# A mixture-of-experts stage: 32 slots in four column groups for small experts, three rounds for 129 to 192 tokens, and the expert biases laid over 128 rows

## The chip, the cores and the metric

The kernel runs on one NeuronCore of a Trainium2 chip. The metric is the device time of one execution in microseconds (us). TensorE (PE in the profile) does the matrix products, VectorE (DVE), ScalarE (ACT) and GpSimd (POOL) the rest, and SyncE (SP) issues the DMA transfers.

## What is computed

The input is one sequence of 256 tokens, 1024 wide, in float32. A first block applies a modulated mixer (windowed attention beside a linear recurrence) and then a mixture of experts; two layers of a second kind follow (three attention and pooling branches, then a gated feed-forward). The change touches the mixture of experts alone. Cut to what matters, with `h` the 256 tokens:

```python
logits = h @ w_router + b_router                 # 32 experts
top_vals, top_idx = lax.top_k(logits, 4)         # each token goes to 4 experts
gates = softmax(top_vals)
for each expert e, with the tokens xb that chose it:
    gu   = xb @ w_gu[e] + b_gu[e]                # 1024 -> 2048: gate half, up half
    gate = minimum(gu[:, :1024], 7.0)
    up   = clip(gu[:, 1024:], -7.0, 7.0)
    y    = ((up + 1.0) * gate * sigmoid(1.702 * gate)) @ w_down[e] + b_down[e]
    out[tokens] += y * gates
```

The weights of one expert are 1024 x 2048 and 1024 x 1024 float32 numbers, 12.58 MB. How many tokens an expert gets depends on the inputs. The reference's router, run on these inputs, gives for experts 0 to 31: 23, 7, 42, 55, 16, 24, 146, 18, 11, 55, 31, 4, 12, 57, 6, 15, 59, 61, 7, 52, 22, 9, 2, 52, 31, 1, 19, 75, 38, 26, 11, 37. So 20 experts have at most 32 tokens, ten have 33 to 64, expert 27 has 75 and expert 6 has 146.

## The kernel before

Every engine runs a program of its own, in an order written out by hand, and waits on semaphores. The mixture of experts is a loop over the 32 experts on PE, ACT, DVE and SP.

**Slots and rounds.** The tokens of an expert get slots 0, 1, 2, ... A round handles 64 slots (`FEW`). PE, ACT and DVE read the expert's count (`value_load`, L1093 on PE) and branch: one round for at most 64 tokens, two for at most 128, four for more. A semaphore that counts rounds goes up by `R // rounds` with `R` = 4, so that an expert always adds four.

**One round on PE** (`expert`, from L998). It begins with the bias (L1009): four products per round that write the whole of banks 0 (gate) and 1 (up). `bias_hi` and `bias_lo` hold the biases of 32 experts times two column halves over 64 rows, split into a high and a low part in the rounded type fp32r, and `bias_sel` picks the expert's rows. Then come the gate and up products (L1017): for each of 8 pieces `gu0` to `gu7` of the weights (1 MB each), for gate and up, two products of 64 slots by 512 columns, one into the first 64 partitions of the bank, one into the other 64. Each takes a different half of the weight columns, and they use different column groups of the array. A float32 product shows as two MATMUL rows. Then the middle: the previous expert's result is added into the accumulators (`combine`, L994), the gates are transposed (L1034), the next tokens are gathered (L980), the hidden values are transposed (L1050, four transposes) and the gathered tokens too (L987). Last comes the down product (L1068), 16 products of 64 by 512 over the pieces `dn0` to `dn3` (1 MB each).

**Around it.** ACT computes the sigmoids and copies banks to SBUF (L1490 to L1505). DVE clips and multiplies gate and up (L1939 to L1955, operations 256 columns wide), copies the transposed hidden values (L1958), and prepares selection tables for the next expert (`select`, `select_gates`, `select_bias`).

**The weights.** SP loads them into a ring of 12 slots of 1 MB, which is exactly one expert (`load_expert`, L630 for gate and up, L632 for down). A slot is refilled with the same piece of the next expert once PE has used it in the expert's **last** round:

```python
if final and k < DT - 1:
    last.then_inc(gu_used.sem, 1)        # PE, in the last round only
```

After the last expert the same queue loads the first weights of the next layer (8.3 MB) into slots that come free.

**Bias set-up.** Before the loop, SP loads the bias rows with two transfers (L619), ACT copies them rounded into `bias_hi` (L1466), DVE makes `bias_lo` (L1832).

Of the kernel before, what the change touches and what calls it, by code (L numbers as in the profile page):

```python
# [22 lines left out]
P = 128  # L23
T = 256
# [15 lines left out]
FEW = 64  # L40
LIMIT, ALPHA = 7.0, 1.702
# [9 lines left out]
ROUNDS = 4  # L51

# [108 lines left out]

def constants():
# [67 lines left out]
def build(nc, dram, out, stop=None):  # L230
# [12 lines left out]
    with ctx:  # L243
# [14 lines left out]
        bias_hi, bias_lo = sb("bias_hi", [P, 2, 512], F32R), sb("bias_lo", [P, 2, 512], F32R)  # L258
# [118 lines left out]
        bias_raw = lru_a.rearrange("p a b -> p (a b)")[0:2 * NE, :].rearrange("p (a b) -> p a b", a=2)  # L377
# [183 lines left out]

        block = ctx.enter_context(nc.Block())
# [3 lines left out]
        def _(sp):  # L566
# [183 lines left out]
        def _(pe):  # L750
# [220 lines left out]
            both = (slice(0, FEW), slice(FEW, P))  # L971

# [25 lines left out]
            def expert(e, rounds):  # L998

                u = R // rounds  # L1000
                for r in range(rounds):
                    final = r == rounds - 1

                    pe.wait_ge(xT_ready.sem, xT_ready.at(R + r * u, e))
                    if r == 0:
                        pe.wait_ge(sel_ready.sem, sel_ready.at(1, e))
                    for g in range(2):
                        for n, rows in enumerate((bias_hi, bias_lo)):
                            mm(psum[g], bias_sel[0:2 * NE].rearrange("p a b -> p (a b)"), rows[0:2 * NE, g, :], start=n == 0,  # L1009
                               stop=False, skip_group_check=True)  # L1010
                    for k in range(DT):
                        if r == 0:
                            pe.wait_ge(exp_in[f"gu{k}"].sem, exp_in[f"gu{k}"].at(16, e))
                        wt = piece(exp_stream, f"gu{k}", 2).rearrange("p g (c f n) -> p g c f n", f=2, n=P)
# [11 lines left out]
                    pe.wait_ge(y_ready.sem, y_ready.at(R + r * u, e))  # L1026
                    pe.wait_ge(sg_ready.sem, sg_ready.at(R + r * u, e))
# [16 lines left out]
                    pe.wait_ge(sg_ready.sem, sg_ready.at(R + (r + 1) * u, e))  # L1044
                    for h in range(2):
                        if h == 1:
                            pe.wait_ge(up_taken.sem, up_taken.at((r + 1) * u, e))
# [1292 lines left out]
```

## Time and profile before

| | us |
|---|---|
| median of 3 runs | 2229.58 (2224.77 to 2230.18) |
| profiled execution, its own time | 2224.29 |
| its span, first to last instruction | 2222.5 |
| PE busy | 2122.2 (95%) |
| DMA queue, share of the 16 engines | 67.9% |
| mean granted TensorE clock | 0.989 |

The span lies 1.8 us under the execution's own time. "Busy" counts an engine as busy while one of its instructions runs; PE is pipelined, so a busy PE is not PE at its peak. In the 40 slices of the page, the experts fill slices 4 to 22 (about 180 to 1240 us), and the GB/s row there reads 381 418 417 303 1 381 418 and on to 411. Numbers that the page gives for the whole span average over stages of very different kinds, so the prediction reads each stage by itself.

### The profile page before, as it was taken

What the parts mean: (1) busy time and instruction counts of PE and PEld (TensorE: products, weight loads), DVE (VectorE), ACT (ScalarE), POOL (GpSimd) and SP (SyncE); (2) the same over time, 40 slices, a digit from 0 to 9 for tenths busy, and PEclk for the clock granted to TensorE, in tenths of its full rate; (3) what the DMA queues carried; (4) which work ended last, traced back from release to release, by engine and by line L of the source; (5) the groups of instructions that cost most, each with busy time, mean ns of one, the idle gap of its engine ahead of it and who ended that gap; (6) DMA issues with size and microseconds to landing.
All of it is one profiled execution on the core that took longest, in us unless ns stands there. A gap on an engine that the chain in (4) does not pass through costs nothing.

```text
span 2222.5 us, 29751 instructions
## 1 busy us (share of the span) xinstructions
PE 2122.2 (95%) x11486; PEld 1333.1 (60%) x11487; DVE 812.7 (37%) x1468; ACT 540.9 (24%) x905; POOL 25.3 (1%) x45
## 2 busy tenths in 40 slices
PE   6998999999999999999999999999999999999999
PEld 4763333333333333333333787778999887688999
DVE  3521221122222112221121348434885258425874
ACT  1421111111111111111111122312663132403653
POOL 0000000000000000000000020000000020000000
PEclk8998999999999999999999999999999999999999
DMA  9686997099999999999899334316551633325551
GB/s 347 254 353 255 410 419 303 1 381 418 418 417 417 417 419 418 418 418 418 334 417 411 106 114 152 114 40 199 178 194 53 199 112 118 114 97 169 190 176 53
DMA packets 210004, 580.05 MB, mean 261 GB/s; under 512 B 23264, under 2 KB 124896, under 8 KB 173952
## 3 DMA queue, kind: packets, MB, share of 16 engines
q1 hardware_dynamic: 209920, 578.83, 67.9%
q8 instruction: 65, 1.06, 0.2%
q14 instruction: 19, 0.16, 0.0%
HBM read 577.48 MB, written 1.31 MB: 260 GB/s over the span
## 4 chain that ended last, share of the span: by engine, by line
PE 69%; DMA 10%; SPq 8%; DVE 8%; ACT 3%; issue 2%; ACTq 0%; DVEq 0%
PE bank L756 16%; PE bank L1017 13%; DMA ring<-in_w_gu 9%; PE bank L1068 8%; SPq L630 4%; SPq L632 4%; PE bank L1340 3%; PE bank L1342 3%; PE bank L1341 3%; PE bank L980 3%; PE bank L994 3%; DVE heap L2104 2%; PE bank L826 2%; DMA ring<-in_w_in 2%; PE bank L1356 1%
## 5 line engine op out<-in xcount | busy, mean ns | idle before, releaser
L1017 PE MATMUL bank<-ring,heap 128*64 128x512 f32 x2304 | 519.2, 601 | 23.9 <-DMA ring<-in_w_gu 23.8
L1017 PEld LDWEIGHTS bank<-ring,heap 128*64 128x64 f32 x2304 | 158.0, 138 | 367.2 <-issue 289.2
L756 PE MATMUL bank<-heap,ring 128*128 128x256 f32 (+1 forms) x1600 | 350.5, 380 | 5.3 <-DVE heap L2148 3.2
L756 PEld LDWEIGHTS bank<-heap,ring 128*128 128x128 f32 (+1 forms) x1600 | 301.0, 189 | 51.5 <-DVE heap L2148 4.0
L1939 DVE TENSOR_SCALAR heap<-bank 128x256 f32<-128x256 f32 x36 | 15.3, 425 | 744.9 <-PE bank L1017 744.9
L1068 PE MATMUL bank<-ring,heap 128*64 128x512 f32 x1152 | 255.1, 595 | 0.0
L1340 PE MATMUL bank<-h_hi,w_hi 128*128 128x256 f32 x640 | 181.7, 284 | 3.4 <-DVE w_lo L2161 3.4
L1342 PE MATMUL bank<-h_hi,w_lo 128*128 128x256 f32 x640 | 181.1, 283 | 0.0
L1341 PE MATMUL bank<-h_lo,w_hi 128*128 128x256 f32 x640 | 181.1, 283 | 0.0
L2161 DVE TENSOR_TENSOR w_lo<-ring,w_hi 128x2048 fp32r<-128x2048 f32 (+1 forms) x64 | 142.4, 2226 | 97.7 <-ACT w_hi L1635 97.7
L1068 PEld LDWEIGHTS bank<-ring,heap 128*64 128x64 f32 x1152 | 79.3, 137 | 150.2 <-issue 144.2
L1491 ACT ACT_TABLE_LOAD x32 | 41.1, 1283 | 485.5 <-DVE heap L1939 485.0
L1635 ACT ACTIVATE w_hi<-ring 128x2048 fp32r<-128x2048 f32 (+1 forms) x64 | 119.1, 1861 | 145.2 <-PE bank L1342 85.5
L1340 PEld LDWEIGHTS bank<-h_hi,w_hi 128*128 128x128 f32 x640 | 122.8, 192 | 3.9 <-DVE w_lo L2161 3.8
L1341 PEld LDWEIGHTS bank<-h_lo,w_hi 128*128 128x128 f32 x640 | 122.8, 192 | 0.1
L1342 PEld LDWEIGHTS bank<-h_hi,w_lo 128*128 128x128 f32 x640 | 122.8, 192 | 0.0
L1356 PE MATMUL bank<-f_hi,w_hi 128*128 128x256 f32 x352 | 100.0, 284 | 1.0 <-DVE w_lo L2161 1.0
L1357 PE MATMUL bank<-f_lo,w_hi 128*128 128x256 f32 x352 | 99.6, 283 | 0.0
L1358 PE MATMUL bank<-f_hi,w_lo 128*128 128x256 f32 x352 | 99.6, 283 | 0.0
L1505 ACT ACTIVATE heap<-bank 128x512 f32<-128x512 f32 x36 | 21.5, 598 | 231.5 <-PE bank L1068 231.5
L980 PE MATMUL bank<-heap 128*64 128x512 f32 x296 | 73.4, 617 | 3.5 <-DVE heap L1899 3.5
L994 PEld LDWEIGHTS bank<-heap 64*128 64x128 f32 x592 | 54.1, 186 | 35.8 <-issue 29.2
(299 smaller groups left out, 2321.9 us busy)
## 6 DMA issues: line engine op xcount, KB each, us to landing
ring<-in_w_gu SPq DMA_DIRECT2D x256, 1024.0 KB, 18.8
ring<-in_w_down SPq DMA_DIRECT2D x128, 1024.0 KB, 19.8
ring<-in_ffn_w_up SPq DMA_DIRECT2D x44, 1024.0 KB, 7.7
ring<-in_w_ada SPq DMA_DIRECT2D x24, 1024.0 KB, 10.6
ring<-in_w_in SPq DMA_DIRECT2D x24, 1024.0 KB, 7.9
ring<-in_ffn_w_down SPq DMA_DIRECT2D x16, 1024.0 KB, 6.0
ring<-in_w_in SPq DMA_DIRECT2D x7, 2048.0 KB, 12.2
ring<-in_w_out SPq DMA_DIRECT2D x6, 2048.0 KB, 12.8
```

What stands on the lines that cost most here:

```text
L756: last = mm(outp, w(k), x(k), start=k == 0, stop=k == nk - 1)
L980: last = mm(psum[2][both[f], :], pick[:, t, FEW * r:FEW * (r + 1)], htok[:, t, 512 * f:512 * (f + 1)], start=t == 0, stop=t == TT - 1)
L994: last = mm(acc_of(f, c), y_sb[both[f], P * c:P * (c + 1)], sgT[both[f], :], start=False, stop=True, skip_group_check=True)
L1017: last = mm(psum[g][both[f], :], xgT[:, k % 4, k // 4, :], wt[:, g, :, f, :], start=False, stop=k == DT - 1, skip_group_check=True)
L1068: last = mm(psum[2][both[f], :], hidT[:, o:o + FEW], wt[:, 512 * f:512 * (f + 1)], start=k == 0, stop=k == DT - 1)
L1340: mm(b[:, g, :], wh, h_hi[:, k, :], start=k == 0, stop=False)
L1341: mm(b[:, g, :], wh, h_lo[:, k, :], start=False, stop=False)
L1342: last = mm(b[:, g, :], wl, h_hi[:, k, :], start=False, stop=k == DT - 1)
L1356: mm(b[:, a, :], wh, f_hi[:, k, :], start=k == 0 and a == 0, stop=False, skip_group_check=True)
L1357: mm(b[:, a, :], wh, f_lo[:, k, :], start=False, stop=False, skip_group_check=True)
L1635: f(hi, src, ACT.Copy).then_inc(S["whi"].sem, 1)
L2161: v.tensor_tensor(lo, src, hi.bitcast(F32), ALU.subtract).then_inc(S["wlo"].sem, 1)
```

## The change

It has four parts.

1. Experts with at most 32 tokens get a branch of their own: 32 slots. Gate and up are computed by four products of 32 slots by 256 columns, each in a column group of its own (`quarter`), in place of two of 64 by 512. The bias of such an expert is made by eight float32 products of 256 columns. The hidden values then lie in 256 columns of 128 partitions and not in 512, so ACT and DVE work on 128 columns at a time and PE makes two transposes in place of four. The down product has 32 slots per product, and as many products and columns as before.
2. Experts with 129 to 192 tokens take three rounds (`turns` gives the semaphore steps 1, 1, 2) and not four.
3. The biases' high and low parts lie one above the other in one tile `bias_pair` of 128 rows, so that one product per bank adds both: two per round in place of four. It takes four bias transfers in place of two, and four small copies per expert in `select_bias` in place of two.
4. The branching is one helper, `by_count`, for the three engines, with the small counts first.

```diff
+FEWER = 32
+CLASSES = ((32, 1), (64, 1), (128, 2), (192, 3), (256, 4))
...
+def turns(rounds):
+    marks = {1: (0, 4), 2: (0, 2, 4), 3: (0, 1, 2, 4), 4: (0, 1, 2, 3, 4)}[rounds]
+    return [(r, a, b - a) for r, (a, b) in enumerate(zip(marks, marks[1:]))]
...
-        bias_hi, bias_lo = sb("bias_hi", [P, 2, 512], F32R), sb("bias_lo", [P, 2, 512], F32R)
+        bias_pair = sb("bias_pair", [P, 2, 512], F32R)
...
+            def among(classes):
+                (most, rounds), rest = classes[0], classes[1:]
+                if not rest:
+                    expert(e, rounds, most <= FEWER)
+                    return
+                with eng.If(n <= most):
+                    expert(e, rounds, most <= FEWER)
+                with eng.Else():
+                    among(rest)
...
-            for f in range(2):
-                sp.dma_start(bias_raw[NE * f:NE * (f + 1)].rearrange("e g (c n) -> e (g c) n", n=P),
-                             bias_rows.rearrange("e (b f n) -> f e b n", f=2, n=P)[f]).then_inc(bias_in.sem, 16)
+            for g in range(4):
+                sp.dma_start(bias_raw[NE * g:NE * (g + 1)].rearrange("e g (c n) -> e (g c) n", n=P),
+                             bias_rows.rearrange("e (b f n) -> f e b n", f=2, n=P)[g % 2]).then_inc(bias_in.sem, 16)
...
             both = (slice(0, FEW), slice(FEW, P))
+            quarter = [slice(FEWER * j, FEWER * (j + 1)) for j in range(4)]
...
                     for g in range(2):
-                        for n, rows in enumerate((bias_hi, bias_lo)):
-                            mm(psum[g], bias_sel[0:2 * NE].rearrange("p a b -> p (a b)"), rows[0:2 * NE, g, :], start=n == 0,
-                               stop=False, skip_group_check=True)
+                        if few:
+                            for f in range(2):
+                                for c in range(2):
+                                    mm(psum[g][quarter[2 * f + c], 0:T], bias_sel[:, f, 0:FEWER].bitcast(F32),
+                                       bias_pair.bitcast(F32)[:, g, :].rearrange("p (i c n) -> p i c n", c=2, n=P)[:, :, c, :],
+                                       start=True, stop=False, skip_group_check=True)
+                        else:
+                            mm(psum[g], bias_sel.rearrange("p a b -> p (a b)"), bias_pair[:, g, :], start=True, stop=False,
+                               skip_group_check=True)
...
                             for f in range(2):
-                                last = mm(psum[g][both[f], :], xgT[:, k % 4, k // 4, :], wt[:, g, :, f, :],
-                                          start=False, stop=k == DT - 1, skip_group_check=True)
+                                if few:
+                                    for c in range(2):
+                                        last = mm(psum[g][quarter[2 * f + c], 0:T], xgT[:, k % 4, k // 4, 0:FEWER],
+                                                  wt[:, g, :, c, f, :], start=False, stop=k == DT - 1, skip_group_check=True)
+                                else:
+                                    last = mm(psum[g][both[f], :], xgT[:, k % 4, k // 4, :],
+                                              wt[:, g, :, :, f, :].rearrange("p i c n -> p (i c) n"),
+                                              start=False, stop=k == DT - 1, skip_group_check=True)
...
+                    wide = 1 if few else 2
...
-                        for i in range(2):
+                        for i in range(wide):
...
+                        n = FEWER if few else FEW
                         for f in range(2):
-                            last = mm(psum[2][both[f], :], hidT[:, o:o + FEW], wt[:, 512 * f:512 * (f + 1)],
+                            last = mm(psum[2][FEW * f:FEW * f + n, :], hidT[:, o:o + n], wt[:, 512 * f:512 * (f + 1)],
...
-            v.tensor_tensor(bias_lo[0:2 * NE], bias_raw, bias_hi[0:2 * NE].bitcast(F32), ALU.subtract).then_inc(bias_ready.sem, 1)
+            v.tensor_tensor(bias_pair[2 * NE:P], bias_raw[2 * NE:P], bias_pair[2 * NE:P].bitcast(F32), ALU.subtract) \
+                .then_inc(bias_ready.sem, 1)
...
                 for f in range(2):
-                    ins = v.tensor_copy(bias_sel[0:2 * NE, f, :],
-                                        const("ident")[0:2 * NE, bass.ds(e + NE * f, 1)].to_broadcast([2 * NE, FEW]))
+                    for half in (slice(0, 2 * NE), slice(2 * NE, P)):
+                        ins = v.tensor_copy(bias_sel[half, f, :], const("ident", 2 * P)[half, bass.ds(e + NE * f + half.start, 1)]
+                                            .to_broadcast([2 * NE, FEW]))
...
-            def expert(e, rounds):
-                u = R // rounds
+            def expert(e, rounds, few):
+                w = P if few else T
```

How the instructions stand, first on PE at the start of an expert with one round, before (for every expert of at most 64 tokens), rows of one product each:

```order
L1009 MATMUL bank0<-bias_hi,bias_sel 128x512 [waits sel_ready]
L1009 MATMUL bank0<-bias_lo,bias_sel 128x512
L1009 MATMUL bank1<-bias_hi,bias_sel 128x512
L1009 MATMUL bank1<-bias_lo,bias_sel 128x512
L1013 ISA
L1017 MATMUL bank0<-ring,heap 64x512 [waits in_gu0]
L1017 MATMUL bank0<-ring,heap 64x512
L1017 MATMUL bank1<-ring,heap 64x512 x2
```

The same place in the change, for an expert of at most 32 tokens:

```order
L1039 MATMUL bank0<-bias_pair,bias_sel 32x256 [waits sel_ready]
L1039 MATMUL bank0<-bias_pair,bias_sel 32x256 x3
L1039 MATMUL bank1<-bias_pair,bias_sel 32x256 x4
L1047 ISA
L1053 MATMUL bank0<-ring,heap 32x256 [waits in_gu0]
L1053 MATMUL bank0<-ring,heap 32x256 x3
L1053 MATMUL bank1<-ring,heap 32x256 x4
```

A piece of weights takes eight products of 256 columns where it took four of 512, and the wait for the piece stands where it stood. The same place in the change for 33 to 64 tokens, where only the bias differs:

```order
L1043 MATMUL bank0<-bias_pair,bias_sel 128x512 [waits sel_ready]
L1043 MATMUL bank1<-bias_pair,bias_sel 128x512
L1047 ISA
L1056 MATMUL bank0<-ring,heap 64x512 [waits in_gu0]
L1056 MATMUL bank0<-ring,heap 64x512
L1056 MATMUL bank1<-ring,heap 64x512 x2
```

Then on PE the end of the middle and the start of the down product, in the change, for at most 32 tokens:

```order
L1092 MATMUL bank3<-consts_sb,heap 128x128 [waits hid_ready]
L1089 REGISTER_ALU [waits up_taken]
L1092 MATMUL bank1<-consts_sb,heap 128x128 [waits hid_ready]
L1016 MATMUL bank0<-consts_sb,heap 128x128 [waits x_ready,g_ready]
L1016 MATMUL bank0<-consts_sb,heap 128x128 x3
L1112 MATMUL bank2<-ring,heap 32x512 [waits in_dn0,hidT_ready]
L1112 MATMUL bank2<-ring,heap 32x512 x3
```

Each of the two transposes of hidden values was a pair before; the down products keep their number and their 512 columns.

## Rows read from the trace of the kernel before

**Rows 1.** By stretch: busy us (instructions) per engine, PEclk, DMA share, GB/s; the experts' weights.

```profile
core 0: us, PE busy (x) PEld busy (x) DVE busy (x) ACT busy (x) POOL busy (x), PEclk, DMA share, GB/s
188.40:375.70 187.30, 179.01 (x854) 66.58 (x852) 33.56 (x94) 26.41 (x43) 0.00 (x0) 0.97 0.99 403
375.70:448.60 72.90, 72.29 (x360) 27.78 (x358) 12.43 (x32) 8.79 (x18) 0.00 (x0) 1.00 0.01 1
448.60:1083.40 634.80, 605.21 (x2910) 219.35 (x2908) 123.45 (x346) 90.27 (x152) 0.00 (x0) 1.00 1.01 416
1083.40:1092.60 9.20, 9.20 (x44) 3.20 (x42) 0.00 (x0) 0.60 (x1) 0.00 (x0) 1.00 0.00 0
```

**Rows 2.** The same view, one round each: experts 0, 2 and 22.

```profile
181.60:215.00 33.40, 30.00 (x135) 11.12 (x134) 5.70 (x16) 4.19 (x7) 0.00 (x0) 0.91 0.80 320
245.50:273.20 27.70, 27.44 (x136) 10.34 (x134) 5.70 (x16) 4.19 (x7) 0.00 (x0) 1.00 1.02 419
...
907.60:937.80 30.20, 28.27 (x137) 9.99 (x135) 5.70 (x16) 4.19 (x7) 0.00 (x0) 1.00 1.02 418
```

**Rows 3.** Chain of waits, 340 to 480 us (start, length, what): expert 6's last round.

```profile
444.42 1.12 PE bank L1009 x4
445.53 13.88 PE bank L1017 x64
459.42 1.93 PE bank L994 x16
...
465.00 7.02 PE bank L1068 x32
```

**Rows 4.** The same view, 1040 to 1240 us: expert 27, and the last expert's end.

```profile
1048.94 24.86 DMA ring<-in_w_gu
1073.84 1.94 PE bank L1017 x8
...
1088.43 1.13 PE bank L1009 x4
...
1219.75 7.04 PE bank L1068 x32
1226.87 0.61 ACT heap L1505
...
1237.84 2.37 PE bank L1163 x11
```

**Rows 5.** Timeline (start, length) at expert 0: its gate and up products, the first refills.

```profile
183.62 15.60 PE L1017 MATMUL bank<-ring,heap 128*64 128x512 f32 x64
...
187.40 12.33 SPq L630 DMA_DIRECT2D ring<-in_w_gu  x8
```

**Rows 6.** Timeline of PE: products of 256 columns, and the transposes of hidden values.

```profile
1248.03 28.11 PE L756 MATMUL bank<-ring 128*128 128x256 f32 x128
...
264.75 0.66 PE L1050 MATMUL bank<-consts_sb,heap 128*128 128x128 f32 x4
```

**Rows 7.** Timeline of PE: four column groups in the mixer's modulation; short products.

```profile
17.88 3.64 PE L795 MATMUL bank<-ring,vec 128*32 128x512 f32 x32
...
117.30 0.27 PE L893 MATMUL bank<-heap 128*64 128x128 f32 x1
...
117.47 0.27 PE L892 MATMUL bank<-heap 128*64 128x128 f32 x1
```

**Rows 8.** By stretch, columns as in rows 1: the DMA engines before the bias copy.

```profile
133.90:139.10 5.20, 5.20 (x45) 1.97 (x38) 2.88 (x5) 1.31 (x3) 0.00 (x0) 1.00 0.00 1
```

**Rows 9.** Timeline of ACT: the copy of the biases.

```profile
138.70 1.05 ACT L1466 ACTIVATE bias_hi<-heap 64x1024 fp32r<-64x1024 f32 x1
```

**Rows 10.** Waits, 180 to 1240 us: us in total, times, longest.

```profile
PE bank L1009 <- issue: 6.7, 2, 3.5
```

**Rows 11.** By stretch, columns as in rows 1: the modulation, paced by its weights.

```profile
21.60:26.40 4.80, 2.13 (x16) 0.31 (x16) 1.49 (x5) 0.00 (x0) 0.00 (x0) 1.00 1.03 428
26.40:31.60 5.20, 3.87 (x16) 0.40 (x16) 0.00 (x0) 0.36 (x1) 0.00 (x0) 0.51 1.01 381
```

More of the change, by code:

```diff
@@ L996, in combine @@
                 return last
-            def expert(e, rounds):
-                u = R // rounds
-                for r in range(rounds):
+            def expert(e, rounds, few):
+                for r, at, u in turns(rounds):
                     final = r == rounds - 1
-                    pe.wait_ge(xT_ready.sem, xT_ready.at(R + r * u, e))
+                    pe.wait_ge(xT_ready.sem, xT_ready.at(R + at, e))
                     if r == 0:
@@ L1514, in _ @@
             with act.Fori(0, NE) as e:
-                n = act.value_load(counts_i[0:1, bass.ds(e, 1)], min_val=0, max_val=T)
-                with act.If(n > P):
-                    expert(e, 4)
-                with act.Else():
-                    with act.If(n > FEW):
-                        expert(e, 2)
-                    with act.Else():
-                        expert(e, 1)
+                by_count(act, e, expert)
             for i in range(4):
@@ L1925, in _, with expert @@
             v.tensor_copy(small_done, gsum[:, 0, 0:1]).then_inc(slots_ready.sem, 1)
-            def expert(e, rounds):
-                u = R // rounds
-                c = Chain(dve, e_chain, e)
-                for r in range(rounds):
+            def expert(e, rounds, few):
+                w = P if few else T
+                for r, at, u in turns(rounds):
                     final = r == rounds - 1
                     if final:
-                        dve.wait_ge(x_full.sem, x_full.at(R + r * u, e))
+                        dve.wait_ge(x_full.sem, x_full.at(R + at, e))
                         select(e + 1).then_inc(pick_ready.sem, 1)
-                    dve.wait_ge(gate_full.sem, gate_full.at((r + 1) * u, e))
-                    v.tensor_scalar(act_g[:, 0:T], psum[0][:, 0:T], LIMIT, None, ALU.min).then_inc(g_ready.sem, u)
-                    v.tensor_scalar(act_g[:, T:2 * T], psum[0][:, T:2 * T], LIMIT, None, ALU.min).then_inc(g_ready.sem, u)
-                    dve.wait_ge(g_ready.sem, g_ready.at((2 * r + 2) * u, e))
-                    dve.wait_ge(up_full.sem, up_full.at((r + 1) * u, e))
-                    for h in range(2):
-                        part = slice(T * h, T * (h + 1))
+                    dve.wait_ge(gate_full.sem, gate_full.at(at + u, e))
+                    for h in range(2):
+                        part = slice(w * h, w * (h + 1))
+                        v.tensor_scalar(act_g[:, part], psum[0][:, part], LIMIT, None, ALU.min).then_inc(g_ready.sem, u)
+                    dve.wait_ge(g_ready.sem, g_ready.at(2 * (at + u), e))
+                    dve.wait_ge(up_full.sem, up_full.at(at + u, e))
+                    for h in range(2):
+                        part = slice(w * h, w * (h + 1))
                         ins = v.tensor_scalar(act_u[:, part], psum[1][:, part], LIMIT, -LIMIT, ALU.min, ALU.max)
@@ L1965, in _ @@
             with dve.Fori(0, NE) as e:
-                n = dve.value_load(counts_i[0:1, bass.ds(e, 1)], min_val=0, max_val=T)
-                with dve.If(n > P):
-                    expert(e, 4)
-                with dve.Else():
-                    with dve.If(n > FEW):
-                        expert(e, 2)
-                    with dve.Else():
-                        expert(e, 1)
+                by_count(dve, e, expert)
             dve.wait_ge(route_in.sem, 48)
```

73 lines of the change are left out of this document (35 added, 38 removed).

## The prediction

> **What bounds the kernel now.** I read the experts' stage in the view by stretch, because the page's average (PE 95% busy) mixes stages. While the weights of the experts stream, the DMA engines run at their limit: from 448.6 to 1083.4 us their share is 1.01 at 416 GB/s [rows 1]. That stretch holds the weights of 21 experts (7 to 27), so one expert costs the queue 634.8 / 21 = 30.23 us, a piece of 1 MB 30.23 / 12 = 2.52 us. A round on PE takes 27.7 us when all is there, and 30.2 us where PE waits for pieces [rows 2]. So an expert with one round is bound by its weights, and PE is the faster of the two by only 2.5 us.
>
> The reader is to see next where the queue stands still: 72.9 us from 375.7 to 448.6 at 1 GB/s, and 9.2 us from 1083.4 to 1092.6 [rows 1]. The ring holds one expert, and a slot is refilled only in the expert's last round. The first gap is expert 6 with its four rounds, the second expert 27 with two. Twice, then, PE sets the pace: in the gaps, and in the five rounds behind the second gap, 27.7 us each, until the last expert ends at 1226.9 [rows 4].
>
> From this I take a rule for the sum: the end moves by what the gaps of the queue shrink, plus what the tail saves, and a faster round elsewhere is worth nothing, since 30.23 us per expert stays.
>
> **A round in parts.** Expert 6's last round [rows 3]: bias 1.12, gate and up 13.88, middle 465.00 - 459.42 = 5.58, down 7.02 us; with what lies between, 27.6.
>
> **The change, term by term.**
>
> *Gate and up with 32 slots.* 64 products of 256 columns, two MATMUL rows each, four side by side: 32 steps. Four column groups do run side by side here: in the modulation 32 rows of 512 columns take 3.64 us, 0.114 each, where two groups in the experts take 13.88 / 64 = 0.217 [rows 7, 3]. A row of 256 columns takes 28.11 / 128 = 0.22 us alone [rows 6], so 32 x 0.22 = 7.0 us in place of 13.88: -6.9. Above, the bound is 13.9 (no more side by side than today); by the modulation's rate it would be 128 rows x 0.114 / 2 = 7.3. Issue asks for a product's row each 0.055 us; four short rows at 117.30 to 117.47 start 0.057 apart [rows 7] (two more stand between the two shown), so it can just be done in a burst.
>
> *Bias.* Two of the four products of 1.12 us go for 33 slots and more. Half would be 0.56, but part of it is the lead-in, so -0.47, and a round of 27.1 to 27.2. For 32 slots there are eight float32 products, four steps of 0.22 and a start: about 1.05, no change.
>
> *Middle.* Two of four transposes of 0.66 / 4 [rows 6] go: -0.3 at most, DVE and ACT get shorter operations that PE hides already. Down stays at 7.02, for it still has 512 columns. A round of 32 slots is then 27.6 - 6.9 - 0.3 = 20.4 us.
>
> *Start of the stream.* The first refill waits for piece 0 of expert 0, computed at half clock from 183.62 and released at 187.2 [rows 5]. Expert 0 has 23 tokens, so this takes 1.8 us, not 3.6: -1.8. Up to 375.7 the queue needed 187.3 us for 72 pieces, which at 2.52 are 181.4: 5.9 us were lost while PE, in experts 0 and 1 at clock 0.91, released too late [rows 1, 2]. With 20 us rounds for both (7 tokens in expert 1) I leave 0.5 of it: -5.4. The stream now stands still from 368.5.
>
> *Expert 6, three rounds.* Its first round now waits for its weights. A first round that does ends 5.0 us after the stream stands still (1088.4 against 1083.4 [rows 4, 1]), so at 373.5. A middle round of 27.1 brings 400.6; the last round releases piece 0 after bias and a piece, 0.65 + 1.7 us, and the stream runs 1.35 later (444.4 + 1.1 + 1.75 against 448.6 before). It restarts at 404.3, against 448.6: **-44.3**. Of this 27.6 is the round that goes, 0.5 to 1 the bias, the rest the earlier arrival at expert 6.
>
> *Experts 7 to 26.* The queue still needs 634.8 us: 1039.1. No gain, no loss, as long as rounds stay under 30.2.
>
> *Expert 27 and the tail.* Second round at 1044.1, restart at 1044.1 + 3.7 = 1047.8, four more experts 120.9 us: 1168.7, and the last expert ends 5.0 later, at **1173.7**. PE alone would need 1044.1 + 3 x 27.2 + 2 x 20.4 = 1166.5, so the tail changes sides: it now waits for weights. Against 1226.9 this is **-53**.
>
> *What hides the rest.* The two added bias transfers (128 KB each): the engines are idle from 133.9 to 139.1, and ACT's copy runs at 138.7 [rows 8, 9]; cover gone, they would cost at most their own 1 to 2 us. Two more small DVE copies per expert lie under PE's down product. The next layer's weights come behind the last expert's (8.3 MB, 20 us, now 1168.7 to 1188.7); the first of them must be there 11 us after the last expert's end (1237.84 - 1226.87 [rows 4]), at 1184.7, and lands 4 us behind 1168.7. If later pieces were late, I would give it 5 us.
>
> **Sum.** Profiled execution 2224.29 - 53 = 2171.3. The median of the runs, 2229.58, lies 5.3 over that execution, so the median I forecast is **2176.5**.
>
> **Rivals.**
>
> *A. The small rounds are no cheaper in effect: -33.* Then only a round less for expert 6 (27.6) and 0.47 us in some 13 rounds that PE paces (6) remain: -33, 2196. This takes 7 us lost per small expert, and there are two ways. First, four groups do not gain over two; against it stands the modulation's row. Second, PE pauses and then runs slow. Small experts leave it idle: 0.9 us of work per 2.52 us piece. In the modulation PE worked 2.13 of 4.80 us waiting for weights, and then the granted clock was 0.51, the 1.2 GHz level, for the next 5.2 us [rows 11]. So I expect the clock to fall in these experts. What it costs falls in the middle and down part, dense work of 12.6 us; after the idle stretch at 215.0 expert 1's round, at mean clock 0.90, took 30.5 and not 27.7, thus about +3. Such a round ends late by 3, but the next expert has pieces waiting and catches up, since PE has 30.2 us: nearly hidden, 0 to 3 us in all. Only with a further pause does it add up to 7. A pause of about 3.5 us shows before the bias products twice, 6.7 us in all [rows 10], when a branch or the loop's start is first taken; later returns do not show it. The Trainium skill (Runtime: NRT & Kernel Launch, Instruction fetch mechanics) says that a taken branch whose target is not in the current window forces a fetch before execution goes on. By that rule each of the 18 changes of class between experts might pause; the trace before contradicts it for the loop's return, which happens 31 times with two pauses. In parts (3 to 6 us lost) the gain is 50 to 38.
>
> *B. Slower: the clock stays down in small experts.* If the whole small round ran at 1.2 GHz it would take 2 x 20.4 = 41 us, more than the queue's 30.2, and PE would set the pace throughout: 20 x 41 + 10 x 27.2 + 5 x 27.1 = 1228 us against 1045 before (1226.9 - 181.6), +183, 2412. It decides from (1045 - 407) / 20 = 31.9 us per small round on. For it: the clock row of the modulation. Against it: PE then had no idle time left, and in experts 0 and 1 the clock came back within the round [rows 2]. The Trainium skill (TensorE: Matmul & The Clock Gate, Loop structure matters more than you think) describes waiting for a DMA before each burst of products as the loop that makes PE run cold; by it alone all 20 small experts would run so, and the outcome would be B.
>
> *C. Nothing comes of it.* Were few experts small or none over 128 tokens, or were the queue never idle, time would stay at 2229. The 72.9 us gap speaks against the last, and the router's counts against the rest.
>
> **Chances.** Forecast, gain 45 to 60: 0.72. A, with its partial forms, gain 30 to 45: 0.20. B: 0.03. C: 0.02. More gain than 60: 0.03, for nothing in the queue can give it but a faster start. The range takes in the forecast and A's main part: low 2224.8 (the fastest run) - 59 = 2166, high 2229.6 - 36 = 2194. A measurement of this kernel can tell about 0.3%, 7 us, from no change. Faster by more: 0.95; within: 0.02; slower: 0.03.
>
> **What would show it.** In the view by stretch the gap of the queue at expert 6 should be about 36 us (368 to 404), and the one at expert 27 about 9 us. Experts 7 to 26 together should stay at 635 us whatever their class. The gate and up rows of a small expert with its weights there (experts 7 and 8) should take 7 us, starts 0.055 apart; the tail should show waits for in_w_gu, and the last expert should end near 1174. The clock should show 1.2 GHz stretches in small experts. The forecast is wrong if the second gap ends later than 1055, if a small round takes over 27 us without waiting for weights, or if bias products of many experts are preceded by pauses of 3 us.

## The result, and the profile after

The change makes the kernel slower: 2335.51 us (median of 4 runs, 2334.67 to 2336.77) against 2229.59, a ratio of 1.0485 [1.0471, 1.0499] (in brackets, here and below, the 95% interval). The forecast was 2176.5 us. The profiled execution took 2336.77 us, 112.5 more than the one of before, and the last expert now ends at 1339.5 us and not at 1226.9: all of it lies in the experts' stage.

The stage by stretch, cut where the queue of weights stands still, as in [rows 1]:

```profile
core 0: us, PE busy (x) PEld busy (x) DVE busy (x) ACT busy (x) POOL busy (x), PEclk, DMA share, GB/s
190.80:403.90 213.10, 170.92 (x1144) 63.97 (x1137) 35.02 (x116) 27.25 (x47) 0.00 (x0) 0.90 0.90 356
403.90:441.80 37.90, 37.70 (x183) 13.57 (x184) 4.50 (x12) 4.12 (x8) 0.00 (x0) 1.00 0.00 1
441.80:475.80 34.00, 23.42 (x122) 8.77 (x122) 6.17 (x18) 2.92 (x6) 0.00 (x0) 0.91 0.94 373
480.50:1184.80 704.30, 544.77 (x3766) 196.76 (x3760) 108.56 (x370) 84.23 (x146) 0.00 (x0) 0.88 0.91 359
1184.80:1193.50 8.70, 8.70 (x42) 2.89 (x40) 0.00 (x0) 0.60 (x1) 0.00 (x0) 1.00 0.02 3
```

The gap at expert 6 did shrink, from 72.9 to 37.9 us, as forecast (36). What broke is the steady rate. In 704.3 us the queue brings 20 experts, 35.2 us each where it was 30.2; its share is 0.91 where it was 1.01. PE is busy for 544.77 / 20 = 27.2 us per expert, where it was 605.21 / 21 = 28.8, so PE is not what holds it.

The queues in that stretch (packets, MB, share of the 16 engines), after:

```profile
q1 hardware_dynamic: 44797, 251.65, 90.3%
q14 instruction: 101, 0.83, 0.3%
q8 instruction: 3, 0.05, 0.0%
```

and before, from 448.6 to 1083.4 us, where nothing stands for queue 14:

```profile
q1 hardware_dynamic: 47035, 264.22, 101.4%
q8 instruction: 3, 0.05, 0.0%
```

So 101 blocks of 8 KB of program code are loaded in 20 experts, five per expert, on an instruction queue that was silent. Whose code it is, the queue's line does not say. A hint stands in VectorE's timeline around one expert's end (start, duration, line, operation, count, idle time before and its releaser):

```profile
582.03 1.00 DVE L1937 TENSOR_SCALAR heap<-consts_sb,heap 128x512 f32<-128x512 f32 x2
582.94 0.79 DVE L1946 CAST bias_sel<-consts_sb 64x64 fp32r x4
595.41 0.62 DVE L1930 TENSOR_SCALAR heap<-consts_sb,heap 128x256 f32<-128x256 f32 x2 [11.68 <-issue]
```

After the loop's return VectorE stands still for 11.68 us and waits for no semaphore; experiment 1 confirms that the code is its own. The waits of the stretch (us in total, times, longest) sum this up:

```profile
DVE heap L1930 <- issue: 247.5, 19, 16.1
PEld bank L1053 <- DMA ring<-in_w_gu: 161.0, 87, 3.9
PE bank L1053 <- DMA ring<-in_w_gu: 100.7, 79, 3.4
PE bank L1056 <- DMA ring<-in_w_gu: 47.3, 45, 2.3
```

VectorE's standstill is 247.5 / 19 = 13.0 us at the mean. PE waits for weights, and weights come later. The records of the landings show in what way: each piece of 1 MB lands in 16 parts. In one piece (issued at 568.50 us) the first part lands at 576.37, the fifteenth at 576.94 and the last at 590.70; before, a piece in the steady stretch (issued at 915.92) had its first at 934.01 and its last at 935.93. So one part of the 16 is behind, by 10 to 17 us in most pieces of the stretch, and PE can begin a piece only when its last part is there. Last landings follow each other by 2.5 us (median), as before, by 3.5 us where one code block is fetched between them, and by 4.4 where two are.

PE's small round itself came out as forecast. Expert 1, with its weights there, then an expert paced by its weights:

```profile
212.58 7.09 PE L1053 MATMUL bank<-ring,heap 128*32 128x256 f32 x128
...
595.18 1.42 PE L1053 MATMUL bank<-ring,heap 128*32 128x256 f32 x16 [3.29 <-DMA ring<-in_w_gu]
597.66 1.94 PE L1053 MATMUL bank<-ring,heap 128*32 128x256 f32 x16 [1.06 <-DMA ring<-in_w_gu]
601.18 1.94 PE L1053 MATMUL bank<-ring,heap 128*32 128x256 f32 x16 [1.58 <-DMA ring<-in_w_gu]
```

The 64 products take 7.09 us where two column groups took 13.88 [rows 3]. In the paced expert a piece takes 1.94 us of work in place of 7.09 / 8 = 0.9: the granted clock is 0.50, the 1.2 GHz level, from 600 to 610 us (0.88 on the mean of the whole stretch). This is hidden behind the wait for the next piece.

### The profile page after: what moved, and what is told of

It reads as the page before. It is cut to its first block, busy times and chain, and to the rows that moved or that the text cites. A ratio compares the mean times of both kernels' runs of the same rounds, so it can differ in the third digit from the quotient of the medians.

```text
span 2335.0 us, 32573 instructions
## 1 busy us (share of the span) xinstructions
PE 2041.2 (87%) x12802; PEld 1302.9 (56%) x12803; DVE 797.8 (34%) x1524; ACT 532.8 (23%) x899; POOL 25.4 (1%) x45
## 4 chain that ended last, share of the span: by engine, by line
PE 53%; DMA 20%; SPq 14%; DVE 7%; issue 3%; ACT 2%; ACTq 0%; DVEq 0%
DMA ring<-in_w_gu 19%; PE bank L784 16%; SPq L660 7%; SPq L658 6%; PE bank L1112 5%; PE bank L1056 3%; PE bank L1377 3%; PE bank L1379 3%; PE bank L1378 3%; DVE heap L2128 2%; PE bank L854 2%; PE bank L1023 2%; PE bank L1009 2%; PE bank L1053 2%; DMA ring<-in_w_in 1%
## 5 line engine op out<-in xcount | busy, mean ns | idle before, releaser
L1053 PE MATMUL bank<-ring,heap 128*32 128x256 f32 x2560 | 228.5, 498 | 129.6 <-DMA ring<-in_w_gu 129.5
L1056 PE MATMUL bank<-ring,heap 128*64 128x512 f32 x960 | 230.3, 616 | 64.6 <-DMA ring<-in_w_gu 62.1
L1112 PE MATMUL bank<-ring,heap 128*32 128x512 f32 (+1 forms) x1120 | 248.8, 595 | 3.3 <-DMA ring<-in_w_down 3.2
L1053 PEld LDWEIGHTS bank<-ring,heap 128*32 128x32 f32 x2560 | 87.1, 133 | 263.3 <-DMA ring<-in_w_gu 204.7
L1971 DVE TENSOR_SCALAR heap<-bank 128x128 f32<-128x128 f32 (+1 forms) x70 | 21.1, 343 | 499.4 <-PE bank L1053 269.6
L1056 PEld LDWEIGHTS bank<-ring,heap 128*64 128x64 f32 x960 | 63.4, 139 | 223.9 <-DMA ring<-in_w_gu 118.0
L1112 PEld LDWEIGHTS bank<-ring,heap 128*32 128x32 f32 (+1 forms) x1120 | 67.8, 121 | 158.8 <-issue 144.7
L1930 DVE TENSOR_SCALAR heap<-consts_sb,heap 128x256 f32<-128x256 f32 x66 | 20.3, 350 | 378.9 <-issue 377.6
```

The lines of the kernel that those rows point to most:

```text
L1053: last = mm(psum[g][quarter[2 * f + c], 0:T], xgT[:, k % 4, k // 4, 0:FEWER], wt[:, g, :, c, f, :], start=False, stop=k == DT - 1, skip_gr ...
L1112: last = mm(psum[2][FEW * f:FEW * f + n, :], hidT[:, o:o + n], wt[:, 512 * f:512 * (f + 1)], start=k == 0, stop=k == DT - 1)
```

## The experiments

**The theories.** Three causes are possible. F: VectorE's loop over the experts has become too long to be kept, so every expert fetches it again, and these fetches slow the weights. In the compiled programs the loop has 199 instructions before and 336 after (ScalarE 112 and 176, PE 1950 and 3174). P: PE's longer code, or its branches, make PE late. S: the small rounds are slow, by the low clock or by four products side by side. If F holds, then by what: the traffic of the fetches (F1), or VectorE's standstill of some 13 us per expert (F2)?

**1. Only VectorE longer.** The kernel before, with a branch in VectorE's loop that is never taken; a second run has two. PE's program is that of before.

```diff
-                with dve.If(n > P):
+                with dve.If(n > T - 1):
                     expert(e, 4)
                 with dve.Else():
-                    with dve.If(n > FEW):
-                        expert(e, 2)
+                    with dve.If(n > P):
+                        expert(e, 4)
...
```

> The kernel before, with one branch added to VectorE's loop that is never taken (four more rounds of code for a count of 256, which no expert has). Nothing that is executed changes but one compare and branch. VectorE's loop grows from 199 to 288 instructions and still lies within three blocks of 128. Theory F (VectorE's loop has outgrown what its sequencer keeps, its code is fetched again for every expert, and each fetch delays one of the 16 DMA engines that carry the weights): no change if three blocks fit, 2229 us, about 19 packets on instruction queue 14. Rival C (the low TensorE clock and the pauses of small experts make the changed kernel slow): 2229 us, no change. It is the control for the next run.

> The kernel before, with two such branches that are never taken: VectorE's loop has 377 instructions and reaches over four blocks of 128, as in the changed kernel (336). No small experts, no four column groups, four rounds for expert 6, old biases. Theory F: slower, about 5 us for each expert that waits for weights, 2330 to 2390 us; 60 to 160 more packets on instruction queue 14; the landings of one weight piece spread over 10 us instead of 2. Rival C: 2229 us, since nothing of the small experts is in it.

Measured: 2355.41 us, ratio 1.0584 [1.0559, 1.0610], with 288 instructions in the loop, and 2356.51, 1.0581 [1.0561, 1.0600], with 377. The first was meant as a control without a change, and that expectation failed. Its stretch of 21 experts and its queue 14:

```profile
462.80:1199.30 736.50, 618.78 (x2910) 214.23 (x2908) 123.57 (x346) 90.12 (x152) 0.00 (x0) 1.00 0.91 360
...
q14 instruction: 105, 0.86, 0.3%
```

736.5 / 21 = 35.1 us per expert, with PE's clock at 1.00 and no small round anywhere. This alone reproduces the loss, and P and S fall as its cause; experiment 5 is the test from the other side. The second dead branch adds nothing, and nothing to the fetches either: 105 packets in the same stretch. It adds to VectorE's standstill, though. That is 16.1 us per return at the mean in the first run and 19.4 in the second, at the same time per expert, which speaks against F2.

**2. Where the limit lies.** Dead branches with fewer rounds (239 and 264 instructions), and the changed kernel made shorter on VectorE: `select_gates` and `select_bias` once behind the branches in place of once in each (289), that with one copy in `select_bias` in place of four (283), and the change without its 32-slot class (292).

> The kernel before with one dead branch of one round in VectorE's loop: 239 instructions, between the 199 that keep the code and the 288 that do not. Theory F: either 2229 us or about 2350 us, and nothing between; if what is kept is two blocks of 128, or 256 instructions, it is fast.

> The kernel before with one dead branch of two rounds in VectorE's loop: 264 instructions. Theory F with a limit of 256 instructions: slow, about 2350 us and some 170 packets on queue 14. If both this and the one of 239 are slow, the limit lies below 239; if both are fast, above 264.

> The changed kernel, with the last lines of VectorE's expert (gate table and bias selection of the next expert) moved behind the branching, so that they stand in its program once and not five times. The same instructions are executed in the same order. VectorE's loop shrinks from 336 to 289 instructions, three blocks of 128. Theory F: the fetches go (about 20 packets on queue 14), the stream returns to 416 GB/s, and the time is that of the prediction, 2165 to 2185 us. Rival C: the small experts are as they were, so 2320 to 2336 us.

> The changed kernel with the tail of VectorE's expert once behind the branching and the bias selection as one copy. VectorE runs code of its own for small experts, as in the change; its loop has 283 instructions, between 264 (fast) and 288 (slow). Theory F: either about 2190 us with 19 packets on queue 14 or 2335 us with some 175; nothing between.

> The changed kernel without the class of at most 32 tokens: such experts go through the round of 64 slots. Three rounds for expert 6 and the biases over 128 rows stay. VectorE's loop has 292 instructions, three blocks. Both theories expect it to be fast, so it does not tell them apart alone; it prices the other two parts: 2229.6 - 33 = 2196 us. Had the bias over 128 rows or the three rounds been at fault, it would stay at 2300 us or more.

| run | VectorE's loop | packets, queue 14 | us | ratio |
|---|---|---|---|---|
| p3_dead_239 | 239 | 19 | 2227.09 | 1.0005 [0.9993, 1.0017] |
| p4_dead_264 | 264 | 19 | 2229.54 | 1.0011 [0.9996, 1.0025] |
| s1_283 | 283 | 176 | 2339.15 | 1.0502 [1.0480, 1.0524] |
| t1_tail_once | 289 | 175 | 2336.85 | 1.0502 [1.0484, 1.0519] |
| n1_no_small | 292 | 174 | 2335.69 | 1.0496 [1.0475, 1.0517] |

A step, not a slope, between 264 and 283 instructions. Four expectations had put it wrongly: one took the limit for 256 (p4_dead_264), three for more than 288, 289 and 292 (p1_dead_branch, t1_tail_once, n1_no_small), since they counted on three blocks being kept. The Trainium skill (Runtime: NRT & Kernel Launch, Instruction fetch mechanics) gives most engines a store of 32 KiB, 512 instructions, refilled in blocks of 16 KiB; by its length of 336 instructions the changed loop would fit. The runs have blocks of 8 KB on queue 14 and the step below 283, and they decide.

**3. ScalarE.** Four dead branches in its loop (308 instructions, 196 of them jumped over), then 200 executed instructions more (waits that are satisfied; 312).

> The kernel before with dead branches in ScalarE's loop and none in VectorE's: 308 instructions where it had 112. If the limit is one of every sequencer and the damage is done by the fetches on the weights' DMA engines: slow, 2300 us or more, and some 100 to 170 packets on queue 14, though VectorE never waits. If the damage came from VectorE's own pauses, or if ScalarE keeps more: 2226 us.

> The kernel before, with 200 executed instructions (satisfied waits) at the top of ScalarE's loop: 312 instructions, all but the branches of other classes executed, where a1_scalar_dead had 308 of which 196 were jumped over. If the limit is the same for every engine and the dead code's place made the difference: about 175 packets or more on an instruction queue, an expert at 35 us, total 2340 to 2400. If ScalarE keeps more than VectorE: about 20 packets and 2229 to 2250, since ScalarE only loses the time of its waits (200 at 0.03 to 0.06 us, most of it while it idles).

Measured: 2227.78 us, 1.0000 [0.9987, 1.0013], and 2235.24, 1.0043 [1.0025, 1.0060]; 21 packets on queue 14 in both. ScalarE keeps a loop of this length, where VectorE's is fetched again. Whether ScalarE keeps more is not shown by this. The loops begin at different places of the code: ahead of VectorE's stand 171 to 173 instructions in all these kernels, ahead of ScalarE's 110 (counted before compiling). If what is kept goes by whole blocks, the place of the loop counts as well as its length, and one rule could serve both engines. No run moved a loop. The 9 us of the second are probably the time of its waits, which was not looked into.

**4. By traffic or by standstill.** For the standstill without fetches, VectorE works where it would pause; for the fetches without a standstill that anybody waits for, GpSimd, idle in this stage, runs through a long loop. A short one is its control.

```diff
+            def idle(e, a, b):
+                for i in range(a, b):
+                    v.tensor_reduce(out=junk[:, i:i + 1], in_=consts[:, 0:960], axis=AX.X, op=ALU.max).then_inc(junk_chain.sem, 1)
+                    dve.wait_ge(junk_chain.sem, junk_chain.at(i + 1, e))
...
+            with pool.Fori(0, NE) as e:
+                pool.wait_ge(y_ready.sem, y_ready.at(R, e))
+                for _ in range(900):
+                    pool.wait_ge(slots_ready.sem, 2)
```

(The first part is d1_work_for_pause, the second g1_pool_fetch, whose control g2_pool_short has 300 waits. Two such waits make one instruction: 454 in the loop, 154 in the control.)

> The kernel before, with work on VectorE where the changed kernel's VectorE pauses: six reductions of 960 columns (about 1 us each) at the top of each expert, five behind the class branch, ahead of select_gates. VectorE's loop has about 243 instructions, under the 264 that still ran without fetches. Theory F1 (the fetches of 8 KB hold up one of the DMA engines that carry the weights, and VectorE's own standstill is covered): no fetches, about 20 packets on the instruction queue, an expert stays at 30.2 us in the stretch after expert 6, total 2229 within 10 (late selection tables can cost a few us at experts 6 and 27). Theory F2 (it is VectorE's standstill of 11 us per expert that PE and then the ring wait for, the fetches' traffic is harmless): the same 11 us per expert are there, so an expert takes 35 us and the total is 2340 to 2355.

> The kernel before, with a loop on GpSimd through the experts' stage, once per expert (it waits for the previous expert's y_ready): 450 waits that are already satisfied, 454 instructions, and nothing waits for GpSimd. No other engine's program changes. Theory F1 (traffic of the fetches): if GpSimd's loop is fetched again for each expert, about 7 blocks of 8 KB, 220 packets in all on an instruction queue, then an expert takes 35 us or more and the total is 2345 to 2400, though no engine that anybody waits for pauses. Theory F2 (VectorE's standstill): with or without fetches the total stays at 2229. If no fetches appear (GpSimd keeps more), the run tells nothing of F1.

> As g1_pool_fetch, with 150 satisfied waits, a loop of 154 instructions: the control for the loop itself. Both theories: no fetches beyond about 20, total 2229 within 7 us.

Standstill alone: 2217.09 us, 0.9957 [0.9939, 0.9975], thus no loss from 13 us per expert (why it is below 1 is experiment 6). VectorE's timeline there has 13 us of added work per expert:

```profile
577.98 5.89 DVE L1971 TENSOR_REDUCE junk<-consts_sb 128x1 f32<-128x960 f32 x5
...
585.16 7.08 DVE L1971 TENSOR_REDUCE junk<-consts_sb 128x1 f32<-128x960 f32 x6
```

Fetches alone, the stretch of 21 experts (456.5 to 1148.4 us), and the queues in it:

```profile
456.50:1148.40 691.90, 616.41 (x2914) 215.84 (x2912) 123.54 (x346) 90.11 (x152) 0.00 (x0) 1.00 0.95 383
...
q1 hardware_dynamic: 47036, 264.23, 94.6%
q14 instruction: 90, 0.74, 0.3%
```

32.9 us per expert in place of 30.2, by 90 fetches for an engine that nobody waits for. This is just over half of the 5.0 us, and less than the 35 us that were expected. Its total, 2533.14 us (1.1369 [1.1338, 1.1400]), does not belong to the question: GpSimd takes longer than an expert per turn, its loop outlasts the stage, and the next layer waits for it:

```profile
POOL heap L2257 <- issue: 1615.2, 1, 1615.2
PE bank L1230 <- issue: 235.2, 1, 235.2
```

GpSimd's first work there (L2257) begins at 1616 us, and PE stood still for 235.2 us ahead of the pooling product (L1230). The control has 21 packets and 2225.94 us, 1.0001 [0.9988, 1.0014].

So F1 holds and F2 alone does not, in its 13 us. The price of a fetch in this run is (691.9 - 634.8) / 90 = 0.63 us. In the changed kernel it is (704.3 - 604.8) / 101 = 0.99, with 604.8 us for the same 20 experts in v1_small_three below, and in p1_dead_branch (736.5 - 634.8) / 105 = 0.97. The landings price the fetches one by one. In all four stretches the last part of a piece lands 2.5 us after that of the piece before where no fetch lies between. Where one does, it is 3.46 us in the changed kernel and in p1_dead_branch, 3.45 in p2_dead_branches, and 3.14 in g1_pool_fetch. As g1 keeps its 2.5 us without a fetch, GpSimd's own work is not what slows the weights. Nor does the spacing of the fetches make the difference of a third: in g1 those 5 us and those 11 us behind the one before give both 3.15 and 3.14, in p2 those 5 us and those over 12 us behind give 3.44 and 3.46. Why VectorE's fetches cost more than GpSimd's, and whether its pause has a part in it, stays open.

**5. The change with a short loop.** In v1_small_three the small class exists on PE only; VectorE and ScalarE use their 64-slot code for it (`by_count(dve, e, expert, CLASSES[1:])`), with the tail once and the selection in one copy:

```diff
-                for f in range(2):
-                    for half in (slice(0, 2 * NE), slice(2 * NE, P)):
-                        ins = v.tensor_copy(bias_sel[half, f, :], ...
-                return ins
+                return v.tensor_copy(bias_sel[:, :, :], pair_ident[:, :, bass.ds(e, 1)].to_broadcast([P, 2, FEW]))
```

v2_small_shared has it with four rounds for over 128 tokens, v0_three_only with three rounds and no small class, x1_no_fourth is v1 with three rounds for all counts over 128, which saves the four-round branch but would be wrong for an expert with more than 192 tokens.

> The changed kernel with a short VectorE loop of 182 instructions (before 199, changed 336): small experts keep their 32 slots and four column groups on TensorE, but VectorE and ScalarE run the same code for them as for 64 slots (256 columns at a time); the gate table and bias selection stand once behind the branching, the bias selection is one copy; expert 6 has four rounds again. Theory F: about 20 packets on queue 14, stream at 416 GB/s, and small experts are worth their part alone: 28 us less than before by the working of the prediction, 2197 us. Rival C (small experts on TensorE are what is slow, by the clock or by four products side by side): 2300 us or more.

> The same with the class of three rounds, so all that the change wanted; VectorE's loop has 251 instructions. Theory F: if 251 fit in what the sequencer keeps, 2165 to 2180 us (the prediction's 53 us less), if not, 2330 us with some 170 packets on queue 14; it also narrows the limit, which lies between 199 and 288. Rival C: 2300 us or more either way.

> The version with the short VectorE loop (v1_small_three, 2191 us, 34 less than before) without the small experts: all experts of at most 64 tokens take the round of 64 slots; three rounds for expert 6 and the biases over 128 rows stay. Prediction's working: 33 us less than before, about 2192 us, of which 27 the round and 6 the biases; then the small experts add next to nothing in v1_small_three. Rival: the parts add up as in the forecast (33 and 20), and something else took 20 us in v1_small_three; then this one stands at 2200 or above, having lost the same.

> v1_small_three without the branch for more than 192 tokens (it would be wrong for such an expert; none occurs). TensorE's loop has 2085 instructions, before 1950, with that branch 3174. Theory: the pause of 11 us before expert 7 in v1_small_three, of 10.3 us in the changed kernel, is TensorE's own code coming back after a loop too long for its sequencer. Then the pause falls to under 4 us and the time by 5 to 10 us, to 2181 to 2186. If it is something else, such as the wait for expert 7's weights, it stays at 2191.

| run | VectorE's loop | queue 14 | us | ratio |
|---|---|---|---|---|
| v2_small_shared | 182 | 19 | 2214.88 | 0.9938 [0.9918, 0.9958] |
| v0_three_only | 251 | 19 | 2201.76 | 0.9881 [0.9863, 0.9898] |
| v1_small_three | 251 | 19 | 2191.27 | 0.9843 [0.9822, 0.9864] |
| x1_no_fourth | 170 | 18 | 2186.85 | 0.9813 [0.9793, 0.9833] |

PE's program in v1 has the same 3174 instructions in its loop as the changed kernel's, and the time is 144 us lower. All the times with three rounds or small experts lie above what was expected (2197 for v2, 2192 for v0, 2165 to 2180 for v1). The stretches of v1, then PE in the first round of expert 6 (to 375.81, its down product) and at the start of expert 7 (last two rows):

```profile
187.00:371.70 184.70, 159.31 (x1136) 62.90 (x1130) 35.33 (x93) 27.12 (x45) 0.00 (x0) 0.93 1.00 410
371.70:413.70 42.00, 41.60 (x206) 15.23 (x204) 6.57 (x18) 5.10 (x10) 0.00 (x0) 1.00 0.00 1
413.70:448.00 34.30, 23.29 (x118) 8.65 (x114) 5.66 (x15) 2.92 (x6) 0.00 (x0) 0.89 0.93 369
453.10:1057.90 604.80, 516.00 (x3774) 196.42 (x3768) 117.06 (x310) 87.24 (x146) 0.00 (x0) 0.92 1.01 416
```

```profile
350.04 0.73 PE L1044 MATMUL bank<-bias_pair,bias_sel 128*128 128x512 f32 x2 [3.91 <-issue]
350.70 1.24 PE L1057 MATMUL bank<-ring,heap 128*64 128x512 f32 x3
355.32 14.98 PE L1057 MATMUL bank<-ring,heap 128*64 128x512 f32 x61 [3.39 <-issue]
...
375.81 7.09 PE L1113 MATMUL bank<-ring,heap 128*64 128x512 f32 x32
...
448.28 1.94 PE L1040 MATMUL bank<-bias_pair,bias_sel 128*32 128x256 f32 x16 [11.03 <-issue]
449.98 9.01 PE L1054 MATMUL bank<-ring,heap 128*32 128x256 f32 x128
```

The rate is back at 1.01 and 416 GB/s, with 13 small experts among its 20. What is left of the forecast's shortfall is seen here too: PE stands still for 3.91 and 3.39 us on its way into expert 6, and for 11.03 us on its way out, when it waits for nothing the profile shows. Without the code of the fourth class (2085 instructions in PE's loop) the pause on the way out is 2.90 us:

```profile
443.82 1.07 PE L1040 MATMUL bank<-bias_pair,bias_sel 128*32 128x256 f32 x16 [2.90 <-issue]
```

and the stream does not break at 448 us. The medians differ by 4.4 us with intervals that overlap, so the pause is shown, and what it is worth only roughly. The other traces narrow its cause. The pause into expert 7 is 10.15 us in v0_three_only and 10.42 in n1_no_small, both without small experts on PE, and 2.95 in v2_small_shared, with them. So it is not the small round. It is long in the kernels that have the unused four-round branch behind expert 6's code, and whose PE loops are the longest; which of the two does it was not tried.

**6. Where the ring lies.** In d1 the tile `junk`, 64 bytes per partition, lies ahead of the ring and shifts it. The two runs here have that tile and no added instruction, on the kernel before and on v1.

```diff
+        junk = sb("junk", [P, 16])
```

> The kernel before with one unused tile of 64 bytes per partition (junk, as in d1_work_for_pause) declared ahead of the ring, so that the ring, where the weights land, lies 64 bytes higher; no instruction is added. In d1_work_for_pause an expert took 29.8 us in the stream in place of 30.2 and the total fell by 9 us. If the ring's address did that (a weight packet then takes 159 and 309 ns at the 50th and 90th percentile, not 169 and 318): the same here, total about 2217 against 2226. If the work on VectorE did it: total 2226.

> v1_small_three with the same unused tile ahead of the ring. By the address: 32 experts times about 0.4 us, total 2191 - 9 = 2182, ratio about 0.980. If the address does nothing: 2191, ratio 0.984.

Measured: 2218.84 us, 0.9951 [0.9936, 0.9967], and 2177.16, 0.9771 [0.9752, 0.9789]. In the first, 21 experts take

```profile
452.70:1076.90 624.20, 602.32 (x2910) 221.22 (x2908) 123.55 (x346) 90.11 (x152) 0.00 (x0) 1.00 1.01 423
```

29.7 us each. In the built programs the ring begins at byte 43968 of a partition, 192 past a multiple of 256, and with the tile at 44032, which is 172 x 256. So the address did it, and VectorE's 13 us of work in d1 (ratio 0.9957 against 0.9951) cost nothing, which closes experiment 4. v1 with the shift is the best version that holds for any counts: 51 us under before, and 158 under the changed kernel.

## Why the prediction was wrong, step by step

- **The step that failed: "Two more small DVE copies per expert lie under PE's down product."** I counted what VectorE executes and took all its new code as free. In time it was: d1 hides 13 us per expert. But the loop grew from 199 to 336 instructions by the code for two more classes with their tails, of which an expert executes one, and it was no longer kept: with 264 instructions it is, with 283 it is not. What came in place of "lie under" are five fetches per expert on the DMA engines of the weights, 99.5 us in the long stretch alone.
- **Experts 7 to 26: "The queue still needs 634.8 us".** (The 634.8 us hold 21 experts, 7 to 27; the sum uses them so.) This needs a queue with nothing else on its engines. With five fetches per expert it needed 5.0 us more each. The 20 experts of the long stretch make 99.5 us, the four after expert 27 20 (146.0 us from restart to the last end, forecast 125.9), those up to expert 6 35. The last expert ended 165.8 us behind the forecast, so these are 155; the other 11 are expert 6 and 7, below. Not all of the 155 are fetches: v1, without them, ends 20.2 us behind the forecast, which leaves 145.6 us for them.
- **The fetch rule under rival A.** I weighed it as pauses on PE before the bias products, and dropped it since before shows two pauses in 31 returns. That reading was of PE, whose loop was kept, and of a pause as the only price. The rule spoke of the case that came, on another engine; its cost went through the DMA engines. Rival B, which had the 0.03 for a slower kernel, named the right side for the wrong reason: the small rounds did run partly at 1.2 GHz, and v1 has them at the old rate.
- **Right:** gate and up at 7.0 us (7.09); bias 0.65 us for 64 slots (L1044 to L1057 in v1: 0.66), about 1.05 for 32 (0.89); the down product at 7.02 (7.06); three rounds shrink the gap; a second gap of 9 us (8.7); the tail waits for weights.
- **Missed in size, seen in v1, where the rate is intact.** Forecast and v1: stream stops at 368.5 and 371.7, starts again at 404.3 and 413.7, comes to the end of expert 27's weights at 1039.1 and 1057.9; the last expert ends at 1173.7 and 1193.9. Of the 9.4 us at the restart 3.2 are the start, 6.2 expert 6's first round: it ends at 382.9, 11.2 us behind the stop where I put 5.0 by expert 27's, for it begins behind two pauses of PE. The first of them was there to be read before the change: 3.54 us at 359.85, one of the two of [rows 10]. The next 9.2 us are the refills into expert 7, 34.3 us and a break of 5.1 in place of 30.2, with PE's pause of 11.03 inside. Here PE's added code did cost what the prediction feared in rival A, once and not 18 times.
- **Middle:** two transposes less gave nothing: a small expert's middle takes 5.64 us (479.32 to 484.96 in v1), a 64-slot one 5.58 (expert 6) to 5.64 (expert 9), where I put -0.3. The transposes themselves take 0.44 us in place of 0.66, but PE then waits 0.48 us for ScalarE in place of 0.26.

The parts, by medians against before and with VectorE's loop kept: v0 -25 us (three rounds, shorter biases; the forecast's parts gave 33), v2 -11 (small experts; 20), both together -34, where the forecast said -53. The changed kernel's own figure is that gain, less about 144 us for the fetches.

## What to carry to other kernels

Code that is never executed can cost. Before adding a branch to a loop, count the loop's instructions on every engine, and afterwards read the instruction queues in the view of the queues by stretch, where a queue that was silent and now moves a few packets per turn is the sign. Let engines that are idle anyway share one piece of code over several classes, and specialise only the engine that sets the pace. Where a stream is bound by DMA, look for a transfer of another kind on one of its engines: 0.3% of the traffic made an expert 16% longer, since a piece is there only when its last part has landed.

## What the runs showed that I had not expected

- VectorE's loop is kept at 264 instructions and fetched again, five blocks of 8 KB, at 283. ScalarE keeps 312. How much the place of a loop in the code has to do with it was not tried.
- One fetch of 8 KB costs a saturated stream of weights 0.63 us when GpSimd fetches and 0.97 to 0.99 us when VectorE does, whatever their spacing.
- A shift of the ring by 64 bytes makes the same stream faster, 29.7 us per expert in place of 30.2. A packet of the weights' queue then takes 159 and 309 ns at the median and the 90th percentile, not 169 and 318. The shift puts the ring on a multiple of 256 bytes; that this is the property that counts was not tried.
- PE paused 11 us on its way from expert 6 to 7 with 3174 instructions in its loop, 2.9 with 2085 and no four-round branch behind the code of expert 6.
